# Where the last gate projections stand on TensorE, and where a small table lies in SBUF, in a hybrid retention, convolution and expert layer

## The reference

```python
h = rmsnorm(x, n_pre_mix) * (1.0 + sc1) + sh1
q, k, v, g_ret, cb, cc, cx, ga, gb = split(h @ w_in)          # 8 heads, dk 64, dv 128
o, s_f, s_b = bidir_retention(rope(q), rope(k), v, ...)       # chunks of 128 tokens, both ways
y_ret  = (silu(g_ret) * head_norm(o)) @ w_ret_o
y_conv = (cb * short_conv3(cc * cx)) @ w_conv_o
x = x + g1 * rmsnorm((sigmoid(ga) * y_ret + sigmoid(gb) * y_conv) @ w_o, n_post_mix)
aff = softmax(h2 @ w_router); vals, idx = top_k(aff.T, cap)   # 16 experts choose their tokens
hid = silu(xs @ w_gate) * (xs @ w_up)                         # xs: the chosen tokens
y.at[idx].add((hid @ w_down) * vals)
```

## Time and profile before

| what | value |
|---|---|
| median of 3 runs | 2129.67 us |
| profiled execution | 2126.72 us |
| its span | 2125.0 us |
| TensorE matmuls, busy | 2012.0 us, 95% |
| VectorE, busy | 1171.0 us, 55% |
| ScalarE, busy | 751.4 us, 35% |
| share of TensorE in the chain that ended last | 91% |

### The profile page before, as it was taken

How to read it: one execution, slowest core, us unless ns; L and a number is a source line. 1 busy time by engine, 2 the same in 40 slices (tenths; PEclk the granted TensorE clock), 3 DMA queues, 4 the chain that set the end, 5 groups by cost and what they waited for, 6 DMA issues and landing times.

```text
span 2125.0 us, 33140 instructions
## 1 busy us (share of the span) xinstructions
PE 2012.0 (95%) x12899; PEld 1739.5 (82%) x12899; DVE 1171.0 (55%) x1589; ACT 751.4 (35%) x871; POOL 252.3 (12%) x244
## 2 busy tenths in 40 slices
PE   4999999989999999999999994899999999999992
PEld 3898989879999999999999883677777777777772
DVE  5655546466554232323113547777777677777765
ACT  6722221221111111111112333455565555556652
POOL 1010101000000000000000123112311111221102
PEclk9999999999999999999999996899999999999996
DMA  8111102224443111112324748388877888888768
GB/s 314 33 51 46 52 32 74 77 60 141 141 141 112 40 39 49 30 49 73 94 84 153 258 168 330 116 312 308 297 294 260 302 311 312 307 296 294 260 251 308
DMA packets 179318, 364.92 MB, mean 172 GB/s; under 512 B 10564, under 2 KB 99596, under 8 KB 178372
## 3 DMA queue, kind: packets, MB, share of 16 engines
q1 hardware_dynamic: 162736, 311.23, 41.1%
q0 software_dynamic: 16432, 53.01, 8.3%
q10 hardware_dynamic: 100, 0.03, 0.0%
HBM read 321.21 MB, written 43.02 MB: 171 GB/s over the span
## 4 chain that ended last, share of the span: by engine, by line
PE 91%; DVE 4%; DMA 3%; ACT 1%; SPq 1%; issue 1%; POOL 0%; DVEq 0%; ACTq 0%
PE ps L885 11%; PE ps L887 11%; PE ps L886 11%; PE ps L1153 9%; PE ps L1155 8%; PE ps L1157 8%; PE ps L1165 8%; PE ps L907 3%; PE ps L908 3%; PE ps L909 3%; PE ps L956 2%; PE ps L957 2%; PE ps L958 2%; PE ps L1066 2%; PE ps L1068 1%; PE ps L1067 1%
## 5 line engine op out<-in xcount | busy, mean ns | idle before, releaser
L2068 DVE TENSOR_TENSOR e_lo<-raw,e_hi 128x2048 fp32r<-128x2048 f32 x192 | 439.5, 2291 | 109.5 <-ACT e_hi L1533 109.4
L1533 ACT CAST e_hi<-raw 128x2048 fp32r<-128x2048 f32 x192 | 367.3, 1915 | 205.6 <-PE ps L1157 205.6
L885 PE MATMUL ps<-h_hi,w_hi 128*128 128x384 f32 x960 | 322.1, 335 | 0.6 <-DVE w_lo L1652 0.6
L886 PE MATMUL ps<-h_lo,w_hi 128*128 128x384 f32 x960 | 321.1, 334 | 0.0
L887 PE MATMUL ps<-h_hi,w_lo 128*128 128x384 f32 x960 | 321.0, 334 | 0.0
L1652 DVE TENSOR_TENSOR w_lo<-w_raw,w_hi 128x1024 fp32r<-128x1024 f32 x64 | 78.1, 1220 | 212.2 <-ACT w_hi L1281 212.1
L885 PEld LDWEIGHTS ps<-h_hi,w_hi 128*128 128x128 f32 x960 | 180.6, 188 | 8.5 <-issue 6.1
L886 PEld LDWEIGHTS ps<-h_lo,w_hi 128*128 128x128 f32 x960 | 180.5, 188 | 0.0
L887 PEld LDWEIGHTS ps<-h_hi,w_lo 128*128 128x128 f32 x960 | 180.5, 188 | 0.0
L1153 PE MATMUL ps<-e_hi,x_hi 128*128 128x512 f32 x512 | 159.5, 393 | 0.4 <-ACT x_hi L1539 0.4
L1155 PE MATMUL ps<-e_lo,x_hi 128*128 128x512 f32 x512 | 157.7, 389 | 0.0
(11 more groups left out here) (279 smaller groups left out, 3326.4 us busy)
## 6 DMA issues: line engine op xcount, KB each, us to landing
raw<-in_w_gate_dram SPq DMA_DIRECT2D x64, 1024.0 KB, 7.9
raw<-in_w_up_dram SPq DMA_DIRECT2D x64, 1024.0 KB, 14.7
raw<-in_w_down_dram SPq DMA_DIRECT2D x64, 1024.0 KB, 12.5
w_raw<-in_w_in_dram SPq DMA_DIRECT2D x48, 512.0 KB, 4.0
ada_k<-in_w_ada_dram SPq DMA_DIRECT2D x64, 256.0 KB, 2.8
merged_d<-merged POOLq DMA_DIRECT2D x16, 576.0 KB, 3.5
ada<-in_w_ada_dram SPq DMA_DIRECT2D x7, 1024.0 KB, 17.0
ret_part<-merged_d POOLq DMA_DIRECT2D x8, 576.0 KB, 4.1
```

The costliest lines, as they stand in the source:

```text
L885: pe.matmul(out, w_hi[:, slot, k, :], xh, start=(k == 0), stop=False)
L886: pe.matmul(out, w_hi[:, slot, k, :], xl, start=False, stop=False)
L1533: act.copy(e_hi[u % 4][:].rearrange("p k n -> p (k n)"), raw[(u + 8) % 12][:].rearrange("p k n -> p (k n)"))\
L2068: dve.tensor_tensor(e_lo[u % 4][:].rearrange("p k n -> p (k n)"), raw[(u + 8) % 12][:].rearrange("p k n -> p (k n)"), e_hi[u % 4][:].rearr ...
```

## The change

Two things are changed, and both leave the set of instructions as it is.

The first is the order of TensorE's program in the tail of a pair. `gate_block(i, 0)` stood ahead of `turn_tile(i, 8)` and now stands behind `score_tile(i, 7)`; blocks 1, 2 and 3 each move back by one place, and blocks 4 and 5 stay.

The second is the layout. `cond` (64 bytes per partition) moves from behind `state_out` to ahead of `lg`. Everything between the two moves up by 64 bytes: `lg`, `lgt`, `zeta`, `xi`, `gchunk`, `decay`, `s0`, `stats`, `gn6`, `gnmv`, `gnr` and `state_out`, and with `decay` also `x_hi` and `x_lo`, which then start at 192448, 64 past a multiple of 128. `A_S` stays where it was. An assertion on the address of `decay` goes.

```diff
@@ tables in SBUF
         scale1 = const("scale1", [P, KD, 2])
+        cond = const("cond", [P, KD, 2])
         lg = const("lg", [P, 3, HEADS])
         ...
         gchunk = const("gchunk", [P, HEADS])
-
         A_DECAY = off
-        assert (BASE + A_DECAY) % P == 0
         decay = const("decay", [P, HEADS, P])
         ...
         state_out = const("state_out", [P, 2, P])
-        cond = const("cond", [P, KD, 2])
         A_S = off
@@ TensorE, pair(i)
-
-                gate_block(i, 0)
                 turn_tile(i, NT - 1)
                 key_values(i, NT - 1)
                 score_tile(i, NT - 2)
+                gate_block(i, 0)
+                score_tile(i, NT - 1)
+
                 gate_block(i, 1)
-                score_tile(i, NT - 1)
-                gate_block(i, 2)
-
                 pe.wait_ge(sm_ready, NT * i + NT)
                 outputs(i, 0)
                 outputs(i, 1)
+                gate_block(i, 2)
+                outputs(i, 2)
                 gate_block(i, 3)
-                outputs(i, 2)
                 pe.wait_ge(kv_read, (NT - 1) * (i + 1))
                 outputs(i, 3)
```

## The result

The changed kernel takes 2147.7 us, the median of 4 runs (2146.58 to 2148.73), against 2129.21 us for the kernel before. The ratio is 1.0084, with a 95% interval of 1.0063 to 1.0103: 18.5 us slower. The prediction's time was 2133; 2147.7 lies in its range, 2128 to 2172, but in the part that belongs to its first rival. Its likeliest case, order alone and a layout that costs nothing, did not happen; the range holds the result only because it was drawn wide enough for that rival.

The account below looks back on a forecast made before the run. TensorE was taken as the bound, busy 2012.0 of 2125.0 us in matmuls. 2126.72 + 5.9 for the order and 0 for the layout gave 2132.6 us, forecast as 2133 from the runs' spread, range 2128 to 2172.

Parts of the forecast that it names:

- first rival: L1153, L1155, L1157: loads off a multiple of 128 bytes are slow; 11 ns a step, 17 us, total 2150 us; chance 36%.
- likeliest case: Whole kernel: the new order costs 5.9 us and the layout 0, for 2133 us; chance 54%.
- The stall at the transposes of tile 8: Tail of each pair: TensorE waits 1.48 us for VectorE's `qxs`, four times, 5.9 us in all.
- The two waits behind it: After those transposes: state update of tile 8 waits 0.06 us more for the forward state; score of tile 7 waits nothing.
- The order's term: Tails of the four pairs: TensorE's new order costs 5.9 us, ends 5.5 and 6.2.
- The rest of the tail, nothing: Score of tile 8, outputs and the next pair's panel: no new wait, cost nothing; 4.4 us of slack there grows.
- The idle time behind the fourth pair, unchanged: Hand-over after the fourth pair: TensorE still stands 3.15 us, since the chain hangs on gate block 5.
- The clock there: Hand-over behind the fourth pair: the lower clock costs at most 2.2 us, which could come back or be added; taken as 0.
- The layout, "I take 0": 1536 expert-stage matmuls on `x_hi` and `x_lo`: moving their start to 64 past a multiple of 128 costs 0.
- 108 ns of cover: Expert stage: matmul step 227 ns, load step at most 119, so a load could be 108 ns slower before holding matmuls back.
- the four loads of `aff`: L1111: 48-column loads at both alignments last 116 to 163 ns, median 148; taken as speaking for no cost, not proof.
- point of decision: Expert stage: the first rival decides once those matmuls' step grows by 3 ns, taking the total past 0.5% (10.6 us).

Follow-up runs that it names:

- the map: Kernel before plus 48 + 3 groups of 24 matmuls on copies, operands shifted; time not comparable; mean step 226.7 ns at distance 0, 229.3 at 192.

## Why the prediction was right or wrong

**The stall at the transposes of tile 8**: right in place, releaser and kind; forecast 1.48 us a pair, measured 1.42. The forecast let 0.11 us pass from VectorE's `qxs` to the transposes; the trace has 0.05. The run with gate block 0 alone late shows that this place holds the whole cost of the order.

**The two waits behind it**: mis-sized. The prediction gave the state update 0.06 us and the score nothing; by the tail's rows they took 0.34 us, and by the distance between pairs 1.66 - 1.42 = 0.24 remain for all that is not the first wait. It added the release of 0.11 us to the end of the forward state; in the trace the update starts 213.35 - 213.12 = 0.23 us behind that end, for whatever reason. The order's term was 5.9 with an upper end of 6.2 and came out at 6.6 us by the trace, 8.5 (5.3 to 10.9) by the runs.

**The rest of the tail, nothing**: right. Gate block 3 late measured 0.9999, and the last low part of the next panel had more slack, not less, as the change's timeline of VectorE and TensorE shows against the earlier trace rows (247.73 - 240.24 = 7.5 us, where it was 4.4):

```profile
239.05 1.19 DVE L1655 TENSOR_TENSOR p_lo<-w_raw,p_hi 128x1024 fp32r<-128x1024 f32 x1
```

```profile
247.73 0.39 PE L905 MATMUL ps<-p_hi,h_hi 128*128 128x512 f32 x1
```

**The idle time behind the fourth pair, unchanged**: right, 3.15 us in both. The clock there is what the prediction allowed for, and it moved little. From the end of the last gate block to the first product on z, the granted clock was 0.84 before and 0.92 in the profiled execution of the change, and the stretch was 0.45 us shorter; with the order alone it was as long as before. Before, then the change:

```profile
438.35:460.05 21.70, 17.24 (x92) 16.34 (x91) 18.14 (x25) 11.38 (x12) 0.00 (x0) 0.84 0.08 25
```

```profile
445.80:467.05 21.25, 16.65 (x91) 15.79 (x91) 18.19 (x25) 11.60 (x12) 0.00 (x0) 0.92 0.08 25
```

**The layout, "I take 0"**: this is the step that failed, in its mechanism. The term was 0; it cost 9.8 us by the trace and 9.7 by the runs (6.4 to 11.9), more than the order. The reasoning had three faults. It looked only at the length of a load, found 108 ns of cover, and asked how much longer a load may become; the load did not become longer (188 ns) and the cover did not help, because the matmul that streams while the next load runs became longer. It asked how the start stands to a multiple of 128, where only the distance to the other operand counts. And the row that it leaned on, the four loads of `aff`, tested neither: 48 columns, in another format, and a look at the loads' own durations, which do not move even in the slow case.

**The first rival** had the right place (L1153, L1155, L1157), the right count and a fitting point of decision (3 ns), and with 11 ns a step it was within a factor of two of the 6.5 measured. Its time, 2150 us, lies close to the 2147.7, but that is luck: its 17 us for the layout are 7 too many, its term for the order is 0.7 too small, and it starts from an execution 3 us under the median. Its mechanism, a slower load off a multiple of 128, was wrong: a start on a multiple of 256 was just as slow, and a kernel with the tiles shifted off 128 together was as fast as before. With the measured terms the sum reads 2126.7 + 6.6 + 9.8 = 2143.1 for an execution like the profiled one, and 2129.2 + 16.4 = 2145.6 for the median; the 2.1 us that are left to 2147.7 lie inside the interval and are not explained.

On the rules of the Trainium skill: that a load of 128 columns takes an estimated 107 ns ("TensorE: Matmul & The Clock Gate", LDWEIGHTS) is not contradicted by a step of at most 119, but that figure does not say what a load does to the matmul beside it. The lines of 16 bytes ("SBUF — State Buffer", Specifications) would have made shifts of 64 and of 32 free; all but one of the distances off zero cost 6 to 7 ns in the map, and 192 cost 2.6. The measurement decides. The same page's "Who interferes with whom" says that TensorE's two read ports, for the streaming operand and for the load, are independent; here a load slows the stream beside it by up to 7 ns of 227, depending on where the two operands lie.

What stays open: why the distance matters at all (only that it does, and that it repeats after 256 bytes, is shown), why 192 is cheaper, and why two distances in turn cost more than one.

## What to carry to other kernels

Where TensorE is saturated by matmuls that each bring their own load, treat the address of a stationary operand as part of its cost: keep it a multiple of 256 bytes away from the operand that streams against it, as far as this one form shows, and check this again whenever a small table is added ahead of it; an assertion on the distance says more than one on the address. Work whose input is long ready is worth the most directly ahead of a wait on a fresh result, and moving it by one place cost 1.66 us a pair. When an edit "only" moves data, compare a group of matmuls on the moved tile with the same form on an unmoved one, by the step between starts and not by the duration of the loads. Before a difference of a few us between two profiled executions is put down to an edit, look for short stretches at the lower clock: one of them was worth 1.6 us here, a quarter of the order's cost.

## What the runs showed of the hardware

The step of one matmul of the three-pass product, a 128x128 stationary operand against 512 columns with its own load each time, was 226.7 to 227.8 ns at a distance of 0 modulo 256 bytes between the stationary and the streaming operand, 229.3 at 192, and 233.1 to 234.1 at 32, 64, 96, 128, 160 and 224, in one execution. In the kernel 9.8 us of 2125 hung on it. The load's own duration was 188 ns in the slow case as in the fast one. At the lower level of the granted clock (0.50 to 0.55 by stretch) the same matmul stepped 427 ns. Such stretches came behind a wait of 1.3 to 2.1 us, or where TensorE had been busy for only 9 of 25 us, in some executions and not in others. The 3072 matmuls of the context products were not looked at for this, and other formats than the one here were not tried.
